# Who issues the 36 small transfers around a 16x16 triangular solve: ScalarE or GpSimd

## What is computed

```python
a = jnp.where(strict, jnp.einsum("bhncd,bhnsd->bhncs", k_beta, k) * decay, 0.0)
t_inv = lax.linalg.triangular_solve(eye + a, jnp.broadcast_to(eye, a.shape),
                                    left_side=True, lower=True)
u = jnp.einsum("bhncs,bhnse->bhnce", t_inv, v_beta)
w = jnp.einsum("bhncs,bhnsd->bhncd", t_inv, k_beta * jnp.exp(g)[..., None])
```

## Time and profile before

| | us |
|---|---|
| runs, median of 3 | 1485.55 (1484.68 to 1487.13) |
| span of the profiled execution | 1484.3 |
| TensorE busy in it | 1436.3 |
| ScalarE busy | 837.8 |
| GpSimd busy | 77.5 |

### The profile page before, as it was taken

One profiled execution on the slowest core, in us unless ns is written; L12 is line 12 of the kernel. 1 busy time (PEld: TensorE's weight loads), 2 busy tenths in 40 slices (PEclk: granted clock), 3 DMA queues, 4 the chain that ended last, 5 costly groups with the idle time before them and its releaser, 6 DMA issues.

```text
span 1484.3 us, 20392 instructions
## 1 busy us (share of the span) xinstructions
PE 1436.3 (97%) x8107; PEld 1174.5 (79%) x8107; DVE 1015.0 (68%) x1388; ACT 837.8 (56%) x1237; POOL 77.5 (5%) x153
## 2 busy tenths in 40 slices
PE   6999899999999999999999999999989999999998
PEld 4888688878888878788887888887768778788886
DVE  5787677776555676666557666577878887766655
ACT  5646474655445554564445654458767777465443
POOL 5000000000000000000000000000230410000000
PEclk9999899999999999999999999999999999999999
DMA  6533454344655465466555656555533423465652
GB/s 204 170 115 114 131 170 142 114 135 149 192 184 191 170 209 174 156 200 196 178 192 181 198 176 197 181 163 170 164 94 96 119 86 115 149 199 178 197 179 106
DMA packets 166247, 238.78 MB, mean 161 GB/s; under 512 B 19391, under 2 KB 112362, under 8 KB 166154
## 3 DMA queue, kind: packets, MB, share of 16 engines
q1 hardware_dynamic: 155168, 232.03, 48.2%
q0 software_dynamic: 1328, 4.29, 1.0%
q10 hardware_dynamic: 9658, 1.18, 0.5%
HBM read 235.89 MB, written 1.57 MB: 160 GB/s over the span
## 4 chain that ended last, share of the span: by engine, by line
PE 88%; DVE 3%; ACT 2%; DMA 2%; POOL 2%; issue 1%; ACTq 1%; SPq 0%; DVEq 0%; POOLq 0%
PE A L240 16%; PE A L241 15%; PE A L242 15%; PE G L240 5%; PE M L240 5%; PE M L242 5%; PE G L242 5%; PE G L241 5%; PE M L241 5%; PE A L1155 1%; PE G L1076 1%; POOL gdn_gd_Dpart L1993 1%; POOL gdn_gd_Dinv L1995 1%; DVE w_lo L224 1%; PE G L1123 1%
## 5 line engine op out<-in xcount | busy, mean ns | idle before, releaser
L224 DVE TENSOR_TENSOR w_lo<-raw,w_hi 128x1024 fp32r<-128x1024 f32 (+1 forms) x295 | 506.9, 1741 | 173.0 <-ACT w_hi L206 172.3
L206 ACT ACTIVATE w_hi<-raw 128x1024 fp32r<-128x1024 f32 (+1 forms) x295 | 426.8, 1465 | 186.9 <-DMA raw<-in_ffn_w_gate_up 139.1
L240 PE MATMUL A<-w_hi,x_hi 128*128 128x512 f32 (+1 forms) x640 | 261.9, 409 | 11.1 <-ACT gdn_gd_u L2323 5.0
L242 PE MATMUL A<-w_hi,x_lo 128*128 128x512 f32 (+1 forms) x640 | 248.7, 389 | 0.0
L241 PE MATMUL A<-w_lo,x_hi 128*128 128x512 f32 (+1 forms) x640 | 248.2, 388 | 0.0
L240 PEld LDWEIGHTS A<-w_hi,x_hi 128*128 128x128 f32 x640 | 121.5, 190 | 43.3 <-DVE x_lo L384 7.3
L242 PEld LDWEIGHTS A<-w_hi,x_lo 128*128 128x128 f32 x640 | 121.3, 190 | 25.7
L240 PE MATMUL A<-w_hi,ffn_ffn_hT_hi 128*128 128x512 f32 x352 | 138.7, 394 | 0.0
L241 PE MATMUL A<-w_lo,ffn_ffn_hT_hi 128*128 128x512 f32 x352 | 138.4, 393 | 0.0
L241 PEld LDWEIGHTS A<-w_lo,x_hi 128*128 128x128 f32 x640 | 121.7, 190 | 20.9 <-issue 0.7
L627 ACT ACTIVATE ffn_ffn_e<-ffn_ffn_z 128x512 f32<-128x512 f32 x44 | 27.8, 632 | 194.7 <-DVE ffn_ffn_z L661 194.7
(11 more groups left out here) (372 smaller groups left out, 2103.6 us busy)
## 6 DMA issues: line engine op xcount, KB each, us to landing
raw<-in_ffn_w_gate_up SPq DMA_DIRECT2D x176, 512.0 KB, 4.7
raw<-in_ffn_w_down SPq DMA_DIRECT2D x88, 512.0 KB, 4.0
raw<-in_w_in SPq DMA_DIRECT2D x52, 512.0 KB, 4.5
raw<-in_gdn_w_in SPq DMA_DIRECT2D x48, 512.0 KB, 4.5
raw<-in_sc_w_in SPq DMA_DIRECT2D x24, 512.0 KB, 4.4
raw<-in_w_out SPq DMA_DIRECT2D x16, 512.0 KB, 4.5
raw<-in_gdn_w_out SPq DMA_DIRECT2D x16, 512.0 KB, 4.3
raw<-in_w_mem_kv SPq DMA_DIRECT2D x8, 512.0 KB, 7.8
```

The costliest lines, as they stand in the source:

```text
L206: ins = act.activation(net.w_hi[:, v % RING, part], net.raw[:, v % RING, part], ACT.Copy)
L224: ins = dve.tensor_tensor(net.w_lo[:, v % RING, part], net.raw[:, v % RING, part], net.w_hi[:, v % RING, part].bitcast(F32), ALU.subtract)
L240: pe.matmul(out, xh, hi[:, k, c, :], start=start and k == 0, stop=False)
L242: mm = pe.matmul(out, xl, hi[:, k, c, :], start=False, stop=stop and k == nk - 1)
```

## The change

ScalarE's program loses the four kinds of steps, GpSimd's program gains them, at the same places of the same list. On GpSimd `gather` is followed by `solve`, so the two small clears at the head of `solve` now come behind the gather's issue. No data, shape or semaphore count changes.

```diff
@@ class Gdn, pool()
         for step in self.steps:
-            if step[0] == "gather":
-                solve(int(step[1]))
-            if step[0] != "core":
+            kind = step[0]
+            if kind == "blocks":
+                half = int(step[1])
+                self.kk_done(pool, 4 * half + 3)
+                for b in range(8):
+                    at = slice(16 * b, 16 * b + 16)
+                    pool.dma_start(self.blocks_dram[half, b].rearrange("n r c -> r n c"),
+                                  self.MT_all[half][at, :, at]).then_inc(self.blocks_out.sem, 16)
+            elif kind == "gather":
+                half = int(step[1])
+                pool.wait_ge(*self.blocks_out(128 * (half + 1)))
+                if half:
+                    pool.wait_ge(*self.solved(half))
+                pool.dma_start(self.D[:, :, :], self.blocks_dram[half].rearrange("b n r c -> (b n) r c"))\
+                    .then_inc(self.blocks_in.sem, 16)
+                solve(half)
+            elif kind == "solved":
+                half = int(step[1])
+                pool.wait_ge(*self.solved(half + 1))
+                pool.dma_start(self.solved_dram[half].rearrange("b n r c -> (b n) r c"), self.D_inv[:, :, :])\
+                   .then_inc(self.solved_out.sem, 16)
+            elif kind == "spread":
+                half = int(step[1])
+                pool.wait_ge(*self.solved_out(16 * (half + 1)))
+                for b in range(8):
+                    at = slice(16 * b, 16 * b + 16)
+                    pool.dma_start(self.MT_all[half][at, :, at],
+                                  self.solved_dram[half, b].rearrange("n r c -> r n c")).then_inc(self.solved_in.sem, 16)
+            if kind != "core":
                 continue
@@ class Gdn, act()
-            elif kind == "blocks":
...
-            elif kind == "gather":
...
-            elif kind == "solved":
...
-            elif kind == "spread":
...
```

## The result

The changed kernel takes 1488.32 us (median of 20 runs) against 1485.17 for the kernel before (20 runs beside them). The medians lie 3.15 us apart; the ratio is 1.0017, with a 95% interval of 1.0011 to 1.0023, which puts it at some 2.5 us slower. That is small but clear of zero, within the 0.2% (3 us) that I called no change, and the median is 1.6 us above my 1486.7. The profiled execution has a span of 1484.8 us against 1484.3.

What follows compares the result with a forecast made beforehand. TensorE was taken to bound the kernel. First half -0.9 and second half +2.0 gave +1.1 us: 1484.3 becomes 1485.4, plus 1.25 from span to median, 1486.7 us; range 1480 to 1494, the forecast's own 1483 to 1488.5.

Steps and rivals of the forecast that it cites:

- the stall moves: The forecast case: time within 3 us of before, from GpSimd issues of 0.57 to 0.82 us; chance 0.43.
- What bounds the kernel now: TensorE, busy 1436.3 of 1484.3 us; 36 issues fewer on ScalarE gain nothing unless TensorE waits because of them.
- Part 1: First half: TensorE's 5.0 us wait for the evacuation goes, and 2.5 us of slow clock behind it: -7.5 us.
- Part 2, issue: First chain: each GpSimd issue of 256 pieces takes 0.75 us (0.54 to 1.06); last of eight starts 1.75 later.
- the gain would come through: Rival, faster: GpSimd issues at 0.54 us, transfers land like ScalarE's; about -5.8, 1479.8 us; decides below 0.57 us; chance 0.20.
- Part 2, landing: First chain: each small transfer issued by GpSimd lands 0.7 us later than ScalarE's (0 to +1.5).
- The side estimate for a landing of +0.4: Landing priced from the Trainium skill's first-byte figures, +0.4 instead of +0.7; the sum would be about 1.2 us lower.
- Part 2, gather: First chain: the gather's delay is mostly hidden behind weight traffic, +0.6 us at the solve's end (0 to +3.3).
- Part 2, wait: First transpose of gd_U: TensorE waits 4.1 us for group 0's mask; 0.7 more at group 1, 1.8 of slow clock.
- Part 3: Second half: masks of groups 2 and 3 behind eight issues; waits 2.6 and 0.8, less 1.4 saved: +2.0 us.
- Part 4: Second chain gets 6.3 us longer but stays hidden from TensorE, with 2.4 us of cover.
- The rival of descriptor writes held by VectorE: VectorE's L224 keeps GpSimd from writing descriptors for `blocks:0`; some 6 us over both halves, about 1493 us; chance 0.05.

Runs made afterwards that it cites:

- experiments 3: The changed kernel, with ScalarE keeping a bare wait for the solve at the old place of `solved`, ahead of the evacuation: 1487.6 us, ratio 1.0018.
- experiment 6: The changed kernel, with SyncE holding the load of weight `v3` until `spread:0` has landed: 1483.21 us, ratio 0.9982.
- experiment 4: The changed kernel with only the `blocks` transfers back on ScalarE, the other three kinds on GpSimd: 1487.93 us, ratio 1.0021.
- experiment 8: experiment 2 with SyncE holding the load of weight `v3` until `spread:0` has landed, ScalarE issuing everything: 1483.5 us, ratio 0.999.
- experiment 2: The kernel before with `evac:v0:1` moved ahead of `solved:0`, ScalarE still issuing everything: 1485.76 us, ratio 1.0003.
- experiment 5: The order of 1, with core parts `k1` to `t0` of groups 0 and 1 placed later in TensorE's list: 1478.89 us, ratio 0.9956.
- 1: The changed kernel with `blocks:1` placed behind the masks of groups 2 and 3 in GpSimd's list: 1484.47 us, ratio 0.9993.
- experiment 10: experiment 5 with SyncE holding the load of weight `v3` until `solved:0` has landed: 1481.76 us, ratio 0.9976.

## Why the prediction was right, and where it was not

The outcome was the forecast one, the stall moves, and so was its mechanism: the wait at the evacuation goes, the chain becomes longer, and TensorE waits for GpSimd's mask. But the closeness of the number is luck. Several terms were wrong and cancel, and by two of the signs that the prediction itself named it was wrong: an issue of 256 pieces lies outside 0.57 to 0.82, and the gather did not keep its length. In the profiles, the start of one and the same TensorE instruction in the changed kernel less that in the kernel before is, in us: -1.3 at the start of the stage (the two executions differ from their start), -3.0 at 1072.7, -11.1 at 1089.6, -4.4 at the first transpose, -1.9 at 1101.9, -1.0 at 1175, +0.4 at 1281, +0.5 at the end.

- **What bounds the kernel now**, "36 issues fewer on ScalarE are worth nothing by themselves": wrong by 1.3 us. The norm's wait behind L2384 went, because ScalarE no longer issues eight transfers ahead of it. The row was in the view that I read.
- **Part 1** (-7.5): right. The shift shows -8.1, the wait for the evacuation is gone, the clock near 1080 is 1.00.
- **Part 2, issue** (0.75): mis-sized, 0.56 (0.562 to 0.587 over 32 issues), below the 0.57 that I had set as the point where the gain would come through. It did not, so that point was wrong: it stood on the other terms.
- **Part 2, landing** (+0.7 for each): near for the path (+0.6 for `solved` in experiments 3 and 6; at `spread` +0.7 together with the slower issuing, for which I had a term of its own), but the wrong term. I took the landing of `solved` and `spread` from the row of before (1.8 us), and that row was measured in the hole which part 1 removes. `solved` and `spread` grew by 5.5 us and not 3.15. (The side estimate for a landing of +0.4 is off as well: in the prediction's own sum only two landings reach TensorE, which makes 0.6 us and not about 1.2.)
- **Part 2, gather** (+0.6): wrong in sign, -2.4. I had read its 5.7 us as weight traffic, and that was right: it lands with the load. But I took the load's own length as given, and it goes with ScalarE's issues of `blocks` (experiment 4). The two errors cancel: chain +3.95, predicted +3.75.
- **Part 2, wait** (4.1): 6.55, since TensorE came some 2.3 us earlier, counted from the chain's first issue (1.3 from the norm's wait, 0.6 from part 1, the rest in small shifts), and the chain was 0.2 longer. The clock fell as I said; 2.5 us. First half: -0.6, predicted -0.9.
- **Part 3** (+2.0): right in kind, 1.44 and 0.56 of waiting in place of 2.6 and 0.8, and with the 1.5 that went at the waits for L2431 and L2481 about +0.8. The smaller issue price explains it.
- **Part 4** (hidden): right, but its size was wrong. I had the second chain 6.3 us longer; from the first issue of `blocks:1` to the end of the masks of groups 4 and 5 it took 35.8 us before and 34.9 after (they ended at 1181.3, and the next ones waited for TensorE for 7.88 us). I had priced the second half like the first. There ScalarE was busy with other work when `solved:1` had landed (1.7 us) and issued `spread:1` only 4.16 us after `solved:1`; GpSimd, which has nothing else to do, needed 2.69.
- **Not foreseen**: a slow clock behind the 2.4-us stall for L224 near 1279, some 1.5 us. These are the windows from the end of that stall in the kernel before, in the changed kernel, and in experiment 8, in which ScalarE issues everything:

```profile
1278.50:1283.70 5.20, 4.84 (x21) 4.04 (x22) 4.77 (x4) 0.43 (x1) 0.00 (x0) 1.00 0.54 175
1277.30:1282.50 5.20, 4.76 (x14) 3.78 (x15) 4.85 (x4) 0.07 (x1) 0.00 (x0) 0.67 0.53 172
1274.20:1279.40 5.20, 4.84 (x14) 3.87 (x15) 4.78 (x4) 0.00 (x0) 0.00 (x0) 0.67 0.52 168
```

Ten of the twelve profiles have this fall (0.67 or 0.68), only the kernel before and experiment 2 have not. So it does not hang on GpSimd's issuing, and my reading of the earlier trace rows, that a stall of 2.4 us leaves the clock at 1.00, stood on a single row; experiment 6 contradicts it too. What decides between the two stays open. So does the rest between 1.8 us (stage, in the profiles) and some 2.5 (in the medians).

The rival of descriptor writes held by VectorE is out: three L224 ran from 1053.55 for 3.49 us, as long as in the kernel before, beside the first six of eight issues, which took 0.56 to 0.59 each.

A rule that bears on the table is in the Trainium skill (DMA: Bandwidth & Descriptors, section Queues, rings and completion order): each DMA engine takes turns, packet by packet, between the queues that have work for it. By that rule a different issuing engine does not escape the load's traffic, and the traces agree with 5.3 us on the hardware queue and 4.7 to 5.8 on the software queue. That `solved` lands only with the end of the load, and not sooner, is what the traces show beyond it; no run tells why.

## What to carry to other kernels

A transfer's landing time belongs to the traffic beside it: when an edit removes a stall, the loads that the stall held back return, and every landing measured inside the stall has to be priced again from a row in traffic. For a small transfer issued just behind a large load, take what is left of that load. Moving a wait to an idle engine frees the queue behind it, but the chain behind the wait then becomes the bound; look at once for work to put ahead of its first reader (5.6 us here, experiment 5 against 1, for some ten lines of order). Two cures that draw on the same slack don't add up.

## What the runs showed that I had not expected

- A weight load (two transfers of 512 KB) beside it makes a landing of 128 KB three times as long (1.74 to 5.3 us), though the mean rate in that stretch is 223 GB/s and the DMA share 0.68.
- In the first half, where a weight load follows them, ScalarE's eight transfers of 256 pieces of 64 bytes make what is issued behind them late: the load's second transfer lands after 5.9 to 6.6 us instead of 4.5 to 5.3, the gather after 5.1 to 5.9 instead of 2.9 to 3.6. The same eight from GpSimd do not.
- GpSimd's masks and VectorE's L224 stretch each other: 1.26 to 2.25 us, and 1.16 to 2.0, in experiment 10; GpSimd's DMA issues beside L224 are not held. The Trainium skill (SBUF — State Buffer, section Who interferes with whom) says that a VectorE instruction with two SBUF inputs contends with a GpSimd instruction that reads SBUF; the trace agrees.
